# A gather for two experts whose products keep upper and lower rows apart and run among the last down products

## What is computed

```python
def swiglu(h, w_gate, w_up, w_down):
    a = jnp.einsum('bsd,df->bsf', h, w_gate)
    b = jnp.einsum('bsd,df->bsf', h, w_up)
    return jnp.einsum('bsf,fd->bsd', jax.nn.silu(a) * b, w_down)

def moe_swiglu(h, router, w_gate, w_up, w_down):
    logits = jnp.einsum('bsd,de->bse', h, router).astype(jnp.float32)
    vals, idx = lax.top_k(logits, TOP_K)
    gates = jax.nn.softmax(vals, axis=-1)
    combine = jnp.sum(jax.nn.one_hot(idx, N_EXPERTS, dtype=jnp.float32) * gates[..., None], axis=-2)
    y = jnp.zeros_like(h)
    for e in range(N_EXPERTS):
        y = y + combine[..., e:e + 1].astype(h.dtype) * swiglu(h, w_gate[e], w_up[e], w_down[e])
    return y
```

## Time and profile before

| what | us |
|---|---|
| median of 3 runs (lowest, highest) | 1353.39 (1353.07, 1354.71) |
| the profiled execution's own time | 1354.99 |
| its span | 1353.1 |
| TensorE busy, products / weight loads | 1333.0 (99%) / 1066.6 (79%) |
| VectorE busy | 1129.3 (83%) |
| ACT busy | 966.2 (71%) |
| bytes read, mean rate | 431.60 MB, 320 GB/s |

### The profile page before, as it was taken

How to read it: one execution, slowest core, us unless ns; L and a number is a source line. 1 busy time by engine, 2 the same in 40 slices (tenths; PEclk the granted TensorE clock), 3 DMA queues, 4 the chain that set the end, 5 groups by cost and what they waited for, 6 DMA issues and landing times.

```text
span 1353.1 us, 18809 instructions
## 1 busy us (share of the span) xinstructions
PE 1333.0 (99%) x6459; PEld 1066.6 (79%) x6459; DVE 1129.3 (83%) x1000; ACT 966.2 (71%) x904; POOL 13.7 (1%) x26
## 2 busy tenths in 40 slices
PE   9999999999999999999999999999999999999997
PEld 7788888888787777777777777777777778777775
DVE  6585644444556789999999999999999999999998
ACT  6555433344455478888887888888888887888886
POOL 1100000000000000000000000000000000000000
PEclk9999999999999989999999999999999999999999
DMA  9823655555461069999999999999999999999994
GB/s 374 319 73 141 217 186 186 186 186 186 142 226 36 18 250 395 421 422 422 422 402 364 418 422 421 422 422 368 410 422 422 422 421 399 381 421 422 422 422 194
DMA packets 61402, 433.26 MB, mean 320 GB/s; under 512 B 7067, under 2 KB 7242, under 8 KB 10033
## 3 DMA queue, kind: packets, MB, share of 16 engines
q1 hardware_dynamic: 59312, 426.80, 78.6%
q0 software_dynamic: 1888, 5.78, 1.3%
q10 hardware_dynamic: 160, 0.14, 0.0%
HBM read 431.60 MB, written 1.09 MB: 320 GB/s over the span
## 4 chain that ended last, share of the span: by engine, by line
PE 88%; DVE 5%; ACT 2%; DMA 2%; issue 2%; DVEq 0%; ACTq 0%; SPq 0%
PE ps L1506 19%; PE ps L1508 19%; PE ps L1507 19%; PE ps L1926 6%; PE ps L1925 6%; PE ps L1940 3%; PE ps L1941 3%; DVE wlo L930 3%; PE ps L1971 2%; DMA raw<-in_moe_down 2%; PE ps L1859 1%; PE ps L1630 1%; PE ps L1657 1%; PE ps L1967 1%; PE ps L1979 1%
## 5 line engine op out<-in xcount | busy, mean ns | idle before, releaser
L930 DVE TENSOR_TENSOR wlo<-raw,whi 128x2048 fp32r<-128x2048 f32 (+1 forms) x403 | 908.0, 2282 | 101.0 <-PE ps L1508 64.1
L552 ACT ACTIVATE whi<-raw 128x2048 fp32r<-128x2048 f32 (+1 forms) x403 | 765.4, 1916 | 117.3 <-PE ps L1508 46.3
L1506 PE MATMUL ps<-whi,xhi 128*128 128x512 f32 (+1 forms) x880 | 346.9, 394 | 5.2 <-DVE wlo L930 2.6
L1508 PE MATMUL ps<-whi,xlo 128*128 128x512 f32 (+1 forms) x880 | 342.1, 389 | 0.0
L1507 PE MATMUL ps<-wlo,xhi 128*128 128x512 f32 (+1 forms) x880 | 342.1, 389 | 0.0
L1506 PEld LDWEIGHTS ps<-whi,xhi 128*128 128x128 f32 x880 | 165.3, 188 | 44.9 <-DVE wlo L930 6.7
L1508 PEld LDWEIGHTS ps<-whi,xlo 128*128 128x128 f32 x880 | 165.2, 188 | 34.3
L1507 PEld LDWEIGHTS ps<-wlo,xhi 128*128 128x128 f32 x880 | 165.3, 188 | 32.5
L1926 PE MATMUL ps<-wlo,xhi 128*64 128x512 f32 x392 | 155.2, 396 | 0.0
L1925 PE MATMUL ps<-whi,xhi 128*128 128x512 f32 x392 | 153.6, 392 | 0.0
L1506 PE MATMUL ps<-whi,thi 128*128 128x512 f32 x320 | 126.5, 395 | 0.3 <-DVE wlo L930 0.2
(11 more groups left out here) (251 smaller groups left out, 1074.1 us busy)
## 6 DMA issues: line engine op xcount, KB each, us to landing
raw<-in_moe_up SPq DMA_DIRECT2D x112, 1024.0 KB, 9.2
raw<-in_moe_gate SPq DMA_DIRECT2D x112, 1024.0 KB, 9.7
raw<-in_moe_down SPq DMA_DIRECT2D x112, 1024.0 KB, 9.6
raw<-in_ffn_up SPq DMA_DIRECT2D x14, 1024.0 KB, 4.8
raw<-in_ffn_gate SPq DMA_DIRECT2D x14, 1024.0 KB, 4.8
raw<-in_ffn_down SPq DMA_DIRECT2D x14, 1024.0 KB, 4.8
raw<-in_dil_w_in SPq DMA_DIRECT2D x10, 1024.0 KB, 4.8
raw<-in_swa_w_in SPq DMA_DIRECT2D x4, 1024.0 KB, 19.3
```

The source lines that it names most:

```text
L552: act.activation(whi[:, c % HIS, 0:span(c)], raw[:, c % RAW, 0:span(c)], ACT.Copy).then_inc(hi_ready, 1)
L930: dve.tensor_tensor(wlo[:, c % LOS, 0:n], raw[:, c % RAW, 0:n], whi[:, c % HIS, 0:n].bitcast(F32), ALU.subtract).then_inc(lo_ready, 1)
L1506: pe.matmul(dst, ahi, bhi, start=start, stop=False)
L1508: return pe.matmul(dst, alo, bhi, start=False, stop=stop)
```

## The change

The gather no longer sums upper and lower rows. For each row block it makes two sums of two products each, 192 columns wide: `nhi` with [large, small] and `nlo` with [small, large]. They stand in 384 columns of one bank as upper large, upper small, lower small, lower large, and since a one-hot product of an already rounded part is exact, a plain copy is enough: ACT copies two banks at a time, 768 columns, into `gathered`, a region over the old `xhi` and `xlo`; VectorE's part goes. `pick` becomes 320 columns wide and lies in the same region; it takes three instructions a token tile where it took two. The row blocks of the next pair's gather are spread: block 0 ahead of the large downs, 1 and 2 between their two units, 3, 4 and 5 behind them, 6 and 7 between the two units of the small downs. Blocks 4 to 7 take the banks of 0 to 3 again and wait for their copies. The first pair's gather has eight banks and runs in one piece; one warming product behind it goes. The large expert's up and gate products (`large_in`) and the small one's (`small_in`) read `gathered`.

```diff
@@ -195,10 +195,11 @@
         hn = sb("hn", [P, TILES, D])
         with ExitStack() as attending:
             qk = sb("qk", [P, 2, 512], scope=attending)
-        xhi = sb("xhi", [P, KT, SEQ], F32R)
         with ExitStack() as attending:
+            sb("under_xhi", [P, KT, SEQ], scope=attending)
             probsT = sb("probsT", [P, 2, 512], scope=attending)
-        xlo = sb("xlo", [P, KT, SEQ], F32R)
+        xx = sb("xx", [P, 2, KT, SEQ], F32R)
+        xhi, xlo = xx[:, 0, :, :], xx[:, 1, :, :]
         gain = sb("gain", [P, 2, D])
         with ExitStack() as until_routing:
             memkv = sb("memkv", [P, 2, TILES, 512], scope=until_routing)
...
@@ -311,7 +311,8 @@

         B_U, B_G, B_Y = (0, 1), (2, 3), ((4, 5), (6, 7))
         B_UA, B_GA, B_UB, B_GB = 0, 2, 1, 3
-        B_X, B_PUT, B_GATE, B_SC, B_SC_LAST = (0, 1, 2, 3), 4, 5, (4, 5, 6, 7), (0, 1, 2, 3)
+        B_X, B_X_FIRST = (0, 1, 2, 3, 0, 1, 2, 3), (0, 1, 2, 3, 4, 5, 6, 7)
+        B_PUT, B_GATE, B_SC, B_SC_LAST = 4, 5, (4, 5, 6, 7), (0, 1, 2, 3)
         B_LG, B_RANK = (4, 6), 5

         def score_bank(i):
...
@@ -386,8 +387,16 @@

             return MOE0 + PAIR_UNITS * pair + i + 1

-        def two(bank):
-            return ps[:, bank, :].rearrange("p (k t) -> p k t", k=2)
+        GX = 2 * P + 2 * HALF
+        gathered = free(xx[:, 0, 0, 0:1], (GX, KT), (1, GX))
+        LARGE_HI, LARGE_LO = slice(0, P), slice(P + 2 * HALF, GX)
+        SMALL_HI, SMALL_BOTH = slice(P, P + HALF), slice(P, P + 2 * HALF)
+
+        pick = free(xx[:, 1, KT // 2, 0:1], (P + 3 * HALF, TILES), (1, P + 3 * HALF))
+
+        def picks_of(t, odd):
+
+            return pick[:, t, HALF:HALF + P] if odd == 0 else pick[:, t, HALF + P:3 * HALF + P]


         K2 = SWA_IN
...
@@ -783,12 +792,11 @@
             act.activation(rt[:, 160:176], rt[:, 160:176], ACT.Exp).then_inc(top_exp, 1)
             preload(ACT.Silu)

-            def gather_hi(pair):
-
-                for b in range(4):
-                    act.wait_ge(gx_done, 4 * pair + b + 1)
-                    act.activation(xhi[:, 2 * b:2 * b + 2, 0:P + HALF], two(B_X[b])[:, :, 0:P + HALF], ACT.Copy)\
-                        .then_inc(gxhi, 1)
+            def gather_out(pair, n, banks=B_X):
+
+                act.wait_ge(gx_done, 4 * pair + n + 1)
+                b = banks[2 * n]
+                act.activation(gathered[:, 2 * n:2 * n + 2, :], ps[:, b:b + 2, 0:GX], ACT.Copy).then_inc(gx_out, 1)

             def put_out(pair):

...
@@ -828,14 +836,20 @@
                 act.wait_ge(act_b, STEPS * pair + s + 1)
                 act.activation(small_t(0), small_act(), ACT.Copy).then_inc(thi_b, 1)

+            def next_rows(pair):
+
+                for n in range(1, 3):
+                    gather_out(pair + 1, n)
+                act.wait_ge(units_done, pair_unit(pair, PAIR_UNITS - 3))
+                for b in range(2):
+                    y_hi(0, b)
+                gather_out(pair + 1, 3)
+
             def experts(pair, first=False, final=False):


                 r = ROUNDS * pair
                 if not first:
-                    act.wait_ge(units_done, pair_unit(pair - 1, PAIR_UNITS - 3))
-                    for b in range(2):
-                        y_hi(0, b)
                     cut(MOE0 + 1, r)
                     cut(MOE0 + 2, r)
                     act.wait_ge(units_done, pair_unit(pair - 1, PAIR_UNITS - 1))
...
@@ -879,11 +893,13 @@
                     cut(MOE0 + PAIR_UNITS - 1, r)
                 else:
                     cut(MOE0 + PAIR_UNITS - 1, r)
+                    gather_out(pair + 1, 0)
                     small_thi(pair, STEPS - 1)
                     cut(MOE0 + PAIR_UNITS, r)
-                    gather_hi(pair + 1)
-
-            gather_hi(0)
+                    next_rows(pair)
+
+            for n in range(4):
+                gather_out(0, n, B_X_FIRST)
             experts(0, first=True)
             act.wait_ge(pairs_ready, 1)
             middle = act.value_load(jobs_i[0:1, 0:1], min_val=PAIRS - 2, max_val=2 * PAIRS - 2)
...
@@ -1320,9 +1336,10 @@

             def make_pick(t, col):

-                dve.tensor_scalar(pick[:, t, 0, :], iota1, pos[:, t, col(0)], None, ALU.is_equal).then_inc(pick_ready, 1)
-                dve.tensor_scalar(pick[:, t, 1, :].rearrange("p (r s) -> p r s", r=2), free(iota1[:, 0:1], (0, 2), (1, HALF)),
+                dve.tensor_scalar(pick[:, t, 0:HALF], iota1[:, 0:HALF], pos[:, t, col(1)], None, ALU.is_equal)
+                dve.tensor_scalar(picks_of(t, 1).rearrange("p (r s) -> p r s", r=2), free(iota1[:, 0:1], (0, 2), (1, HALF)),
                                   pos[:, t, col(1)], None, ALU.is_equal).then_inc(pick_ready, 1)
+                dve.tensor_scalar(picks_of(t, 0), iota1, pos[:, t, col(0)], None, ALU.is_equal).then_inc(pick_ready, 1)

             for t in range(TILES):
                 make_pick(t, lambda odd: slice(odd, odd + 1))
...
@@ -1364,14 +1381,6 @@
                 dve.wait_ge(put_done, pair)
                 for t in range(TILES):
                     make_pick(t, lambda odd: bass.ds(2 * pair + odd, 1))
-
-            def gather_lo(pair):
-                for b in range(4):
-                    dve.wait_ge(gxhi, 4 * pair + b + 1)
-                    k = slice(2 * b, 2 * b + 2)
-                    dve.tensor_tensor(xlo[:, k, 0:P], two(B_X[b])[:, :, 0:P], xhi[:, k, 0:P].bitcast(F32), ALU.subtract)
-                    dve.tensor_tensor(xhi[:, k, P + HALF:2 * P], two(B_X[b])[:, :, P + HALF:2 * P],
-                                      xhi[:, k, P:P + HALF].bitcast(F32), ALU.subtract).then_inc(gxlo, 1)

             def y_lo(pair, odd):

...
@@ -1469,11 +1478,8 @@
                     cut(MOE0 + PAIR_UNITS - 1, r)
                     small_tlo(pair, STEPS - 1)
                     cut(MOE0 + PAIR_UNITS, r)
-                    gather_lo(pair + 1)

             expert_numbers()
-            cut_upto(MOE0 + 2)
-            gather_lo(0)
             cut_upto(MOE0 + 3)
             combine_gates()
             experts(0, first=True)
...
@@ -1850,31 +1856,29 @@
             pe.matmul(ps[:, B_RANK + 2, 0:NE], ones, sel[0], start=True, stop=False)
             pe.matmul(ps[:, B_RANK + 2, 0:NE], ones, sel[1], start=False, stop=True).then_inc(rank_done, 1)

-            def gather(pair, first=False):
+            def gather(pair, kts, banks=B_X):

                 pe.wait_ge(pick_ready, 4 * pair + 4)
-                for kt in range(KT):
-                    dst = ps[:, B_X[kt // 2], kt % 2 * SEQ:(kt % 2 + 1) * SEQ]
-                    for n, (t, part) in enumerate([(t, part) for t in range(TILES) for part in (nhi, nlo)]):
-                        last = pe.matmul(dst, part[:, t, kt * P:(kt + 1) * P], pick[:, t, :, :], start=n == 0, stop=n == 3)
+                for kt in kts:
+                    for part, picks, dst in ((nhi, slice(HALF, 2 * P), slice(0, GX // 2)),
+                                             (nlo, slice(0, GX // 2), slice(GX // 2, GX))):
+                        for t in range(TILES):
+                            last = pe.matmul(ps[:, banks[kt], dst], part[:, t, kt * P:(kt + 1) * P], pick[:, t, picks],
+                                             start=t == 0, stop=t == 1)
                     if kt % 2 == 1:
                         last.then_inc(gx_done, 1)
-                    if kt == 1 and not first:
-                        pe.wait_ge(up_added, STEPS * pair)
-                    if kt == KT - 3 and not first:
-                        pe.wait_ge(act_b, STEPS * pair)

             def put_turned(pair):

                 for odd in range(2):
                     for t in range(TILES):
                         pe.transpose(ps[:, B_PUT, odd * SEQ + t * P:odd * SEQ + (t + 1) * P],
-                                     pick[:, t, odd, :].bitcast(F32), ident)
+                                     picks_of(t, odd).bitcast(F32), ident)

                 pe.wait_ge(comb_ready, 1)
                 for odd in range(2):
                     for t in range(TILES):
-                        last = pe.matmul(ps[:, B_GATE, odd:odd + 1], pick[:, t, odd, :].bitcast(F32),
+                        last = pe.matmul(ps[:, B_GATE, odd:odd + 1], picks_of(t, odd).bitcast(F32),
                                          comb[:, t, bass.ds(2 * pair + odd, 1)], start=t == 0, stop=t == 1)
                 last.then_inc(put_done, 1)

...
@@ -2030,23 +2044,32 @@
                 with pe.Fori(2, STEPS) as s:
                     step(s)
                 pe.wait_ge(tlo_a, STEPS * pair + STEPS)
-                for i in range(2):
-                    large_out(MOE0 + PAIR_UNITS - 4 + i, r, i, True)
                 if not final:
-                    gather(pair + 1)
+                    gather(pair + 1, (0,))
+                large_out(MOE0 + PAIR_UNITS - 4, r, 0, True)
+                if not final:
+                    pe.wait_ge(up_added, STEPS * pair + STEPS)
+                    gather(pair + 1, (1, 2))
```

(16 more changed lines are left out.)

## The result

| | kernel before | changed kernel |
|---|---|---|
| median, us | 1353.99 (10 runs, 1352.91 to 1355.39) | 1356.91 (10 runs, 1355.48 to 1358.39) |
| profiled execution: own time / span | 1354.99 / 1353.1 | 1356.80 / 1355.0 |
| ratio | | 1.0023 [1.0015, 1.0031] |

The time lies inside the range given (1350.4 to 1357.5), 3.0 us above the forecast of 1353.9 and 0.5 above the upper figure of the rival "the early loads bring nothing" (1356.4). The ratio is just over the 0.2% that counted as no change, and its interval reaches to both sides of it. So the number was covered, and the likeliest story wasn't the true one. Of the 3.0 us, 0.6 is the starting point: the forecast was added to a median of 3 runs, 1353.39, and the 10 runs of the kernel before give 1353.99. Of the change itself +0.5 was forecast and +2.9 came.

The account below looks back on a forecast made before the run. TensorE, VectorE and the loads were taken to run neck and neck, with ACT's cut of the second unit deciding at seams. Seams +2.3 and first gather -1.8 gave +0.5 us on 1353.39: 1353.9, range 1350.4 to 1357.5.

Parts of the forecast that it names:

- the early loads bring nothing: Rival on the first gather's loads: their earlier issue gains nothing, only +2.3 us is left, 1355.7 to 1356.4; chance 0.20.
- the likeliest story: The forecast itself: seams +2.3 us and first gather -1.8 us, so 1353.9, within 1352 to 1355.5; chance 0.47.
- Bound: Expert layer: TensorE, VectorE and loads neck and neck; first pair at the loads' pace (29.82 us a step), later ones at TensorE's (29.25).
- Products and copies: Gather: 192-column products at 0.112 us each, held by the weight load; ACT's 768-element copies at 0.79 us each.
- The seams: Between pairs: the fourth copy stands ahead of ACT's cut of the second unit; 0.8 + 0.8 + 0.7 = +2.3 us.
- 0.1 more: First seam: six picks instead of four ahead of the subtraction TensorE needs at 689.85 us, so 0.1 us more.
- the read of the loop's count: First seam: this load, costing 0.47 us between copy and scaling, follows the fourth copy, putting the cut at 702.1 against 701.39.
- The first gather: First gather: VectorE's cuts and loads go earlier, the stream gets 1.8 us ahead, -1.8 us; ends 0 and -2.3.
- It stays as it is: First gather at the 1.2 GHz clock level (483 to 488): its 6.75 us unchanged, given the floor of a weight load.
- Rival C: First gather's early loads bring nothing, landings following their own issue; only +2.3 us left, 1355.7 to 1356.4; chance 0.20.

Follow-up runs that it names:

- e1: Changed kernel with ACT's cut of the new pair's second unit moved ahead of the gather's fourth copy: 1354.34 us, ratio 0.9999 to the kernel before.
- e6: Changed kernel loading only the first 1024 of 2048 columns of each expert unit: 1353.76 us, ratio 0.9998 to the kernel before.
- e2: Changed kernel, but VectorE waits for all four copies of the first gather before cutting the third unit: 1357.36 us, ratio 1.0027 to the kernel before.
- e3: Kernel before with VectorE's cut of the third unit moved ahead of the first gather's subtractions: 1354.23 us, ratio 1.0003 to the kernel before.
- e4: Changed kernel with extra products of several widths behind its last one; one profile, 6.8 us of low clock, 59.72 us from cut to cut.
- e8: Kernel before, unchanged, run once more for a second profile: span 1351.9 us, 3.4 us of low clock.

## Why the prediction was right or wrong

**Bound, right.** TensorE, VectorE and the loads run neck and neck; halving the loads takes away every step above 29.25 us and 2.8 us of the time (2.9 above 29.25 in the first profile of the kernel before).

**Products and copies, right.** 0.110 a product against 0.112, copies 0.81 us against 0.79.

**The seams, right in cause and size.** +2.3 forecast, 2.5 measured (38.23, 37.92, 37.53), and e1 shows that the whole of it is the place of one copy. The gap ahead of the second large unit was 0.90 us in the row above for 0.6 to 1.0 (by the distance of starts 1.06, 0.70 and 0.70 at the three seams). That the first seam fits so closely is in part luck, since two sizes missed in opposite directions. For the low half of the turned block "0.1 more" was given, because of six picks, and the gather's first products wait for it 0.3, 0.4 and 0 us at the three seams; with halved loads (e6) that wait is 0 at all three, with the same six picks, so the loads make VectorE late there and not the picks. And for the read of the loop's count 0.47 us was added behind the copy; it runs largely beside the copy, and 0.24 passes from the copy's end (699.98) to the cut (700.22).

**The first gather, wrong.** This is the step that failed: "I take the stream as 1.8 us ahead ... -1.8 us". The first links of the chain were read rightly: the cut moved up, the load went out earlier (by 3.7 us, and by 3.1 against the second profile, 492.49), and the first pair's steps fell to 117.55. What was wrong is that the stream's pace in 490 to 520 and the first pair's loss were taken as the kernel's own, and that a microsecond ahead there was counted as one of the whole time:
- The reference point was one execution. A second profile of the kernel before, in which the stretch 490 to 520 already carries 408 GB/s, loses 1.4 us in the first pair and not 2.3.
- What the first pair gained didn't last. The steps above 29.25 sum to 2.9 and 2.3 us in the kernel before, to 2.5, 1.3 and 2.7 in the changed one: 0.4 to 0.5 less on average, with a spread of 1.4 between profiles of one kernel. By the ratios of e2 and e3, where the early loads alone are taken or given, they are worth 0.5 us and nothing, both inside the noise; e2 and e4, at the same clock, lose 2.5 and 2.7. Why the last pair pays in one execution and not in another stays open.

**A term that was missing.** "It stays as it is" was said of the first gather at the low clock. In the same state of the clock that stretch is even 0.2 us shorter (58.35 against 58.54), but whether the low clock lasts 3.4 or 6.8 us was not among the cases, and it is worth 1.2 to 1.5 us.

The accounts close for single profiles. Changed kernel's first against e8, both with 3.4 us of low clock: seams +2.5, steps above 29.25 +0.2, first gather -0.2, and a start that was later by 0.5 already at the cut at 462; together 3.0, and the spans differ by 3.1. For the medians: seams +2.5, loads -0.4, clock about +0.5 (both estimates from few profiles), which makes 2.6 of the 2.9 measured, in an interval of 2.0 to 4.2. Rival C came nearest with its price of the seams alone, 1355.7 to 1356.4, and it had a chance of 0.20 where the forecast had 0.47. Its reason, that a landing follows its own issue, wasn't tested.

## What to carry to other kernels

When work is split off so that one engine alone does it, look where its last piece falls in that engine's queue: here 0.8 us of copying, directly ahead of a cut for which two engines wait, cost more than all that the change saved, and one line moved gave it back. Don't sum a gain out of stretches where one execution was late: if two things run neck and neck, take the reference from a second profile, and ask of every microsecond won in one stretch whether the stream that sets the pace really gets ahead or only stops waiting there. Where the cost of a product is its weight load, narrower products save nothing; halve the weights instead.

## What the runs showed of the hardware

- Products on the gather's operand, each with weights of its own, cost 0.110 us at 192, 128 and 64 columns alike with 128 columns of weights, and 0.060 with 64; between 256 and 384 columns they follow the columns (0.118 and 0.172). Plain f32 at 192 columns costs two records of 0.164 each, so it doesn't meet the floor there.
- The low granted clock at the first gather lasted 3.4 or 6.8 us in the 14 profiles and nothing in between. It was the short one wherever TensorE had taken up its products by 0.11 us after the fall, and the long one wherever it began 0.20 us or more after it. So in this kernel the 0.3 us by which the changed gather begins later can cost 1.2 to 1.5.
- The load stream holds 419 to 422 GB/s in both kernels between seams; with half the bytes it carries 217, the pace at which TensorE uses them.
